# Cached keys in runs of 32 numbers, turned by VectorE in 32x32 blocks, in a hybrid decoder layer

## What is computed

```python
D_MODEL, SEQ, DEC_BATCH, DEC_SEQ, PAST_LEN, PAGE_SIZE = 1024, 512, 8, 4, 256, 128
h = rmsnorm(x, g_mix_pre)
q, k, v, xr, gb, gates = jnp.split(h @ w_in, [...], axis=-1)
k_all = jnp.concatenate([k_past.astype(k.dtype), k], axis=1)
v_all = jnp.concatenate([v_past.astype(v.dtype), v], axis=1)
...                              # logits = q.k * HEAD_DIM**-0.5 + bias; softmax; times v
o_rnn = hseq.astype(x.dtype) * jax.nn.gelu(gb)
merged = jax.nn.sigmoid(gate_a) * (o_attn @ w_pa) + jax.nn.sigmoid(gate_r) * (o_rnn @ w_pr)
x = x + rmsnorm(merged @ w_out, g_mix_post)
x = x + rmsnorm((jax.nn.silu(g_) * u_) @ w_down, g_ffn_post)
return x, k, v, new_conv, h_last
```

## Time and profile before

| | us |
|---|---|
| three runs | 796.84, 793.07, 792.98 |
| median | 793.07 |
| the profiled execution: its time | 796.87 |
| the profiled execution: its span | 795.1 |
| PE busy | 779.7 (98%) |
| DVE busy | 471.5 (59%) |
| ACT busy | 362.0 (46%) |
| POOL busy | 64.4 (8%) |

### The profile page before, as it was taken

The page is one execution under the profiler, slowest core; times in us unless marked ns, Lnnn a source line. Parts: engine busy times, 40 slices in busy tenths (PEclk is TensorE's granted clock), DMA queues, the critical chain, the costliest instruction groups (busy, mean ns, idle before and its releaser), DMA issues.

```text
span 795.1 us, 16472 instructions
## 1 busy us (share of the span) xinstructions
PE 779.7 (98%) x6116; PEld 739.2 (93%) x6116; DVE 471.5 (59%) x737; ACT 362.0 (46%) x628; POOL 64.4 (8%) x149
## 2 busy tenths in 40 slices
PE   8999999999999999999999999999999999999996
PEld 6988998899898899996789999999999999999996
DVE  4655746736646553674567987887777785222223
ACT  6345535625534732234455555455555564223232
POOL 3501102011010110004000000000000010000000
PEclk7999999999999999999999999999999999999998
DMA  7655244335422123625443333333333134223222
GB/s 212 176 167 162 82 119 137 96 106 150 119 79 81 53 80 112 212 80 179 159 137 84 91 114 92 89 91 106 106 106 106 53 130 127 77 74 91 87 58 113
DMA packets 148865, 89.21 MB, mean 112 GB/s; under 512 B 8709, under 2 KB 142297, under 8 KB 148826
## 3 DMA queue, kind: packets, MB, share of 16 engines
q1 hardware_dynamic: 146014, 81.63, 34.9%
q0 software_dynamic: 2576, 6.45, 2.5%
q10 hardware_dynamic: 236, 0.61, 0.3%
HBM read 81.85 MB, written 6.81 MB: 112 GB/s over the span
## 4 chain that ended last, share of the span: by engine, by line
PE 96%; DMA 1%; DVE 1%; ACT 1%; issue 1%; DVEq 0%; SPq 0%; ACTq 0%
PE ps L859 34%; PE ps L1204 26%; PE ps L1269 17%; PE ps L1103 6%; PE ps L1173 3%; PE ps L958 1%; PE ps L972 1%; PE ps L989 1%; PE ps L931 1%; DMA x_tok<-in_x_prompt_dram 1%; PE ps L881 1%; PE ps L1037 1%; PE ps L888 1%; PE ps L1111 1%; PE ps L1002 1%
## 5 line engine op out<-in xcount | busy, mean ns | idle before, releaser
L1818 DVE TENSOR_TENSOR w_lo<-w_raw,w_hi 128x1024 fp32r<-128x1024 f32 (+1 forms) x68 | 80.9, 1192 | 135.5 <-ACT w_hi L1346 135.2
L859 PE MATMUL ps<-xin_hi,w_hi 128*128 128x272 f32 x576 | 126.5, 299 | 0.9 <-DVE xin_lo L1841 0.9
L1346 ACT ACTIVATE w_hi<-w_raw 128x1024 fp32r<-128x1024 f32 (+1 forms) x68 | 69.9, 1030 | 118.7 <-PE ps L1269 82.6
L859 PE MATMUL ps<-xin_hi,w_lo 128*128 128x272 f32 x576 | 120.4, 288 | 0.0
L859 PE MATMUL ps<-xin_lo,w_hi 128*128 128x272 f32 x576 | 120.2, 288 | 0.0
L859 PEld LDWEIGHTS ps<-xin_hi,w_hi 128*128 128x128 f32 x576 | 90.1, 189 | 9.2 <-issue 7.6
L859 PEld LDWEIGHTS ps<-xin_lo,w_hi 128*128 128x128 f32 x576 | 91.0, 189 | 0.0
L859 PEld LDWEIGHTS ps<-xin_hi,w_lo 128*128 128x128 f32 x576 | 90.5, 189 | 0.0
L1269 PE MATMUL ps<-hid_hi,w_hi 128*128 128x272 f32 x352 | 76.0, 291 | 0.4 <-DVE hid_lo L2211 0.4
L1269 PE MATMUL ps<-hid_lo,w_hi 128*128 128x272 f32 x352 | 75.0, 287 | 0.0
L1269 PE MATMUL ps<-hid_hi,w_lo 128*128 128x272 f32 x352 | 74.9, 288 | 0.0
(11 more groups left out here) (340 smaller groups left out, 1766.0 us busy)
## 6 DMA issues: line engine op xcount, KB each, us to landing
w_raw<-in_w_in_dram SPq DMA_DIRECT2D x72, 256.0 KB, 3.1
g_raw<-in_w_gate_up_dram SPq DMA_DIRECT2D x40, 256.0 KB, 4.0
w_raw<-in_w_down_dram SPq DMA_DIRECT2D x40, 256.0 KB, 2.8
u_raw<-in_w_gate_up_dram SPq DMA_DIRECT2D x20, 256.0 KB, 3.0
e_raw<-in_w_gate_up_dram SPq DMA_DIRECT2D x20, 256.0 KB, 4.4
kc<-in_cache_k_dram SPq DMA_DIRECT2D x64, 64.0 KB, 2.1
vc<-in_cache_v_dram SPq DMA_DIRECT2D x64, 64.0 KB, 2.0
wo_raw<-in_w_out_dram SPq DMA_DIRECT2D x12, 256.0 KB, 4.1
```

Source lines behind the costliest of these rows:

```text
L859: mm = e.matmul(ps[:, bank + h, 0:HT], wt[:, kw, :], xt[:, kx, h * HT:h * HT + HT], start=first and wt is wh and xt is xh, stop=last and ( ...
L1346: e.activation((to or w_hi[s])[:, 0:k, :], w_raw[s][:, 0:k, :], ACT.Copy).then_inc(hi_done, count)
L1818: e.tensor_tensor(wl[:, 0:k, :], w_raw[s][:, 0:k, :], wh[:, 0:k, :].bitcast(F32), ALU.subtract).then_inc(lo_done, count)
```

## The change

Cached keys come from memory in another shape. A key DMA now takes its page slice as 4 blocks of 32 numbers by 128 tokens: block b goes to partitions 32b to 32b+31, `kc` is filled 128 x 4 x 32, in runs of 32 numbers (128 B), 512 runs for each DMA where there were 128 of 512 B. DVE turns four pages at once with its own transpose of 32x32 blocks (`keys_turn(f)`, 128x512), straight from `kc` to `kcT`. The first of the four waits for all 16 DMAs (`kc_in`), and in the loop for the last use of `prT` (`pv_done`). `cache_T` on PE and its copies on ACT and DVE are gone.

By this a page's token 4i + a comes to position 32a + i. The value pages are loaded with the same permutation of rows (4 groups of 32 tokens, still in runs of 512 B), and GpSimd copies the bias of the cached positions in that order, in four copies of 128x256 instead of one of 128x1024.

The prompt's keys go from `kT` to `tok` by one DVE transpose of 128x512, not by PE and ACT. Their store has 4 DMAs of 32 partitions in runs of 128 B where it had one in runs of 512 B. The stores wait for one step less of `mi_free`, counters are renumbered, and the semaphore `acc_zero` is replaced by another.

```diff
-            def load_pages(cache, dst, done, it, part):
+            def page_of(cache, it, j):
+                return cache[0].rearrange("n t h d -> n t (h d)")[bass.ds(page[j], 1), :, bass.ds(it * P, P)]
+            def load_keys(it, part):
                 for j in range(8 * part, 8 * part + 8):
-                    src = cache[0].rearrange("n t h d -> n t (h d)")[bass.ds(page[j], 1), :, bass.ds(it * P, P)]
-                    e.dma_start(dst[:, j, :], src.rearrange("o t c -> t (o c)")).then_inc(done, 16)
+                    e.dma_start(kc[:, j, :], page_of(cache_k, it, j).rearrange("o t (b c) -> b (o t) c", c=BLK)
+                                ).then_inc(kc_in, 16)
+            def load_values(it, part):
+                for j in range(8 * part, 8 * part + 8):
+                    e.dma_start(vc[:, j, :], page_of(cache_v, it, j).rearrange("o (i a) c -> a (o i) c", i=BLK)
+                                ).then_inc(vc_in, 16)
...
-                e.wait_ge(mi_free, it * 7 + 4)
+                        load_keys(it + 1, j - 5)
+                e.wait_ge(mi_free, it * 6 + 3)
                 for g, (op, os) in enumerate(((new_k_prompt, new_k_sample), (new_v_prompt, new_v_sample))):
-                    dst = op[0, 0].rearrange("(tt p) h d -> p tt (h d)", p=P)[:, :, bass.ds(it * P, P)]
-                    e.dma_start(dst, tok[:, g, 0:TT, :]).then_inc(kv_out, 16)
+                    if g == 0:
+                        for a in range(4):
+                            dst = op[0, 0].rearrange("(b i) h d -> i b (h d)", i=32)[:, :, bass.ds(it * P + 32 * a, 32)]
+                            src = tok[32 * a:32 * a + 32, g, 0:TT, :].rearrange("p tt (b j) -> p (tt b) j", j=32)
+                            e.dma_start(dst, src).then_inc(kv_out, 16)
...
-            e.tensor_copy(bias_s[:, :, 0:PAST], bias_rev[:, :, DEC_T:DEC_T + PAST][:, :, ::-1]).then_inc(consts, 1)
+            for f in range(PAIRS):
+                src = bias_rev[:, f, DEC_T:DEC_T + PAST][:, ::-1].rearrange("p (n i a) -> p n a i", n=NPG, i=BLK)
+                e.tensor_copy(bias_s[:, f, 0:PAST].rearrange("p (n a i) -> p n a i", n=NPG, i=BLK), src).then_inc(consts, 1)
...
-                def cache_T(f):
-
-                    if f == 0:
-                        e.wait_ge(kc_in, it * 256 + 256)
-                    tp_wait(f)
-                    for n in range(4):
-                        mm = e.transpose(ps[:, T_BANK, n * P:n * P + P], kc[:, 4 * f + n, :], ident[:, :])
-                    mm.then_inc(tp_ready, 1)
...
-                    begin(1); part(1, 0, 4); cache_T(0); part(1, 4, 8)
-                    cache_T(1); begin(2); part(2, 0, 2); cache_T(2); part(2, 2, 4); cache_T(3); part(2, 4, 8); scores_s()
+                    begin(1); part(1, 0, 8)
+                    begin(2); part(2, 0, 6); scores_s(); part(2, 6, 8)
                 else:
-                    begin(0); part(0, 0, 4); cache_T(0); part(0, 4, 8)
-                    begin(1); cache_T(1); part(1, 0, 4); cache_T(2); part(1, 4, 8)
-                    begin(2); cache_T(3); part(2, 0, 5); scores_s(); part(2, 5, 8)
+                    begin(0); part(0, 0, 8)
+                    begin(1); part(1, 0, 8)
+                    begin(2); part(2, 0, 5); scores_s(); part(2, 5, 8)
                 begin(3); scores(3); part(3, 0, 2); probs_T_s(); part(3, 2, 5)
-                tok_prompt(0, vT, 0, 3); probs_T(0); part(3, 5, 8)
-                begin(4); tok_sample(); probs_T(1); scores(2); part(4, 0, 3); tok_prompt(2, kT, 1, 2); part(4, 3, 5)
+                tok_values(); probs_T(0); part(3, 5, 8)
+                begin(4); tok_sample(); probs_T(1); scores(2); part(4, 0, 5)
...
-                e.activation(tok[:, 0, 0:TT, :], ps[:, M_BANK, :].rearrange("p (tt c) -> p tt c", c=P), ACT.Copy
-                             ).then_inc(mi_free, 1)
...
+                def keys_turn(f):
+                    if f == 0:
+                        e.wait_ge(kc_in, it * 256 + 256)
+                        if not first:
+                            e.wait_ge(pv_done, it)
+                    e.transpose(kcT[:, 2 * f:2 * f + 2, :].rearrange("p b k -> p (b k)"),
+                                kc[:, 4 * f:4 * f + 4, :].rearrange("p n c -> p (n c)")).then_inc(kc_turned, 1)
...
                     next_lo(0)
                     parameters()
-                    next_lo(1); cache_copy(1)
-                    k_copy(); cache_copy(3)
+                    keys_turn(0); keys_turn(1)
+                    next_lo(1)
+                    keys_turn(2)
+                    k_copy()
+                    keys_turn(3)
                     next_lo(2)
                 else:
-                    next_lo(0); cache_copy(1)
-                    next_lo(1); cache_copy(3)
-
+                    next_lo(0)
+                    keys_turn(0); keys_turn(1)
+                    next_lo(1)
+                    keys_turn(2); keys_turn(3)
                     next_lo(2)
                     k_copy()
...
+                e.transpose(tok[:, 0, 0:TT, :].rearrange("p tt c -> p (tt c)"), kT[:, 0:SEQ])
                 e.tensor_copy(tok[0:TS, :, TT, :], ps[0:TS, M_BANK, 0:2 * P].rearrange("p (g c) -> p g c", g=2)
```

More of the change, by code:

```diff
@@ L68 @@
 PT_USES = ((3, 0), (3, 1), (2, 0), (2, 1), (1, 2), (0, 2))
-TP_IT = 5 + len(PT_USES)
+TP_IT = 1 + len(PT_USES)
 TILES_IT = 8
@@ L92 @@
 C_ZERO = 8
-C_BIAS = C_ZERO + 1 + DEC_B + 2 * PAIRS
+C_BIAS = C_ZERO + PAIRS + DEC_B + 2 * PAIRS
+BLK = 32
 SERIES = 9
@@ L355, in program @@
         kc_in = sem("kc_in")
+        kc_turned = sem("kc_turned")
         vc_in = sem("vc_in")
@@ L450, in program @@
         ysq_used = sem("ysq_used")
-        acc_zero = sem("acc_zero")
         yt_ready = sem("yt_ready")
@@ L606, in iteration @@
                 if not last:
-                    e.wait_ge(mi_ready, it * 7 + 4)
-                    load_pages(cache_v, vc, vc_in, it + 1, 0)
-                    load_pages(cache_v, vc, vc_in, it + 1, 1)
+                    e.wait_ge(mi_ready, it * 6 + 3)
+                    load_values(it + 1, 0)
+                    load_values(it + 1, 1)
             load(2, 0, wi[:, :, 2 * 512:2 * 512 + P])
             for part in range(2):
-                load_pages(cache_k, kc, kc_in, 0, part)
+                load_keys(0, part)
             load(3, 1, wi[:, :, 3 * 512:3 * 512 + P])
@@ L937, in scores_s @@
                     e.wait_ge(tile_free[1], it * 4 + 2)
-                    e.wait_ge(mi_free, it * 7 + 1)
-                    tp_wait(4)
+                    e.wait_ge(mi_free, it * 6 + 1)
+                    e.wait_ge(kc_turned, it * 4 + 4)
                     e.wait_ge(logits_done, it * 9 + 1)
@@ L977, in probs_T_s @@
                     e.wait_ge(probs_done, it + 1)
-                    tp_wait(4)
+                    tp_wait(0)
                     for n in range(NPG):
@@ L1007, in out_s_T, with tok_values @@
                 def out_s_T():
-                    mi_wait(4)
+                    mi_wait(3)
                     e.transpose(ps[:, M_BANK, 0:P], o_s[:, :], ident[:, :]).then_inc(mi_ready, 1)
-                def tok_prompt(use, src, free, n_free):
-                    e.wait_ge(tile_free[free], it * 4 + n_free)
-                    mi_wait(use)
+                def tok_values():
+                    e.wait_ge(tile_free[0], it * 4 + 3)
+                    mi_wait(0)
                     for tt in range(TT):
-                        mm = e.transpose(ps[:, M_BANK, tt * P:tt * P + P], src[:, tt * P:tt * P + P], ident[:, :])
+                        mm = e.transpose(ps[:, M_BANK, tt * P:tt * P + P], vT[:, tt * P:tt * P + P], ident[:, :])
                     mm.then_inc(mi_ready, 1)
@@ L1029, in rg_gates @@
                         e.wait_ge(logits_done, it * 9 + 10)
-                    count = e.to_reg(it * 7 + (6 + h))
+                    count = e.to_reg(it * 6 + (5 + h))
                     e.wait_ge(consts, 2)
@@ L1394, in gate @@
                     e.activation(halves(dst), two(j % 2), ACT.Tanh, scale=0.5).then_inc(tile_free[j % 2], 1)
-                def cache_copy(f):
-                    e.wait_ge(tp_ready, it * TP_IT + (f + 1))
-                    e.activation(kcT[:, 2 * f:2 * f + 2, :], ps[:, T_BANK, :].rearrange("p (b k) -> p b k", b=2),
-                                 ACT.Copy).then_inc(tp_free, 1)
                 def exp_s():
@@ L2282, in _ @@
             e.wait_ge(q3_done, NS)
-            e.memset(yacc[:, :], 0.0).then_inc(acc_zero, 1)
-            e.wait_ge(acc_zero, 1)
+            e.memset(yacc[:, :], 0.0).then_inc(consts_v, 1)
+            e.wait_ge(consts_v, 4)
             def down_lo(n, odd, c):
```

53 lines of the change are left out of this document (24 added, 29 removed).

## The result

The changed kernel takes 827.13 us (median of four runs, 825.71 to 828.5), the kernel before 793.06. The ratio is 1.041, 95% interval 1.038 to 1.044. The prediction said 848, in a range of 803 to 915.

What follows compares the result with a forecast made beforehand. PE bounds the kernel before (98% busy); after, the queue on four engines: 34.6 us later to iteration 2's key issue, 20.4 for two further periods, less 0.4, is 54.6, so 793.1 becomes 847.7 (848), range 803 to 915.

Steps and rivals of the forecast that it cites:

- engines from the outermost dimension: Key and value loads: a load is spread over its outermost dimension, 4 here, so both run on 4 engines of 16.
- The 43 packets of q10: Queue q10's packets beyond 193 of data, read as completion packets, 16 + 11 + 16, one for each engine a load uses.
- The first wait: Iteration 0, before tile 2: DVE waits for all 16 key DMAs and PE stands idle for 14.6 us.
- its vanishing in the queue: Iteration 0: the 14.6 us are no term of their own, because the four engines stay full from there.
- the waits before tile 0: Loop: PE idle before tile 0, whose weights land 52 us after a key issue; period 74 us against 64.
- before tiles 6 and 7: Loop: PE idle before these tiles too, as their weights queue behind key loads on four engines; period 74 us against 64.
- The price of a 128 B packet: Key loads and stores: 13.5 ns a packet, from a line through 512 B (29.1 ns) and 4096 B (174.9 ns).
- 8.6 us for a nanosecond: Whole kernel: each nanosecond of a 128 B packet adds 8.2 us by four key batches, 8.6 with the stores.
- Rival C: Same queue, but the clock falls after new gaps: tile 0 takes 11.2 us instead of 8.0, time 857; chance 0.15.
- A: Rival: all 16 engines serve the new loads, a key batch takes 6.9 us, hidden; 784.7 us, faster; chance 0.08.
- B: Rival: 128 B packets cost about what 512 B packets cost, 22 ns and more; up to 982 us; chance 0.10.
- D: Rival: PE still stands for something else where groups were removed, so they give nothing; 793 us; chance 0.01.

Runs made afterwards that it cites:

- no_first_wait: Changed kernel, but in iteration 0 DVE turns a gain row instead of the cached keys and waits for no key page; all DMAs stay: 826.2 us.
- best2: Changed kernel, but iteration 0 loads and turns keys as before; values in token order, half issued behind the next iteration's tile 0; DVE writes keys in token order: 786.6 us.
- keys_512B_4: Changed kernel, but a key DMA takes whole rows of 512 B, 128 packets in 4 groups of 32 tokens, on four engines: 801.2 us, ratio 1.009.
- both_16: Changed kernel, but values in token order and keys in whole 512 B rows, both on 16 engines, PE reading cached keys with a stride: 789.5 us, ratio 0.993.

## Why the prediction held, and what was mis-sized

**The step that decided, engines from the outermost dimension, is shown**: by the paces at 16, 4 and 2 engines and by the completion packets. The 43 packets of q10 were enough to tell.

**The signs and places.** The first wait (13.3 against 14.6), its vanishing in the queue, and the waits before tile 0 came as forecast. The waits that the prediction put before tiles 6 and 7 show within the tiles: PE's wait for ACT's `ti` at 93.07 stands behind a `w_hi` that waited 4.95 us for its weights. PE was busy for 94% where 91% was forecast.

**The price of a 128 B packet was too high: 13.5 ns.** Eight key DMAs in 9.69 us are 1.21 each, 9.5 ns for each of 128 packets; in the first batch, 22.65 / 16 gives 11.1. By the prediction's own 8.6 us for a nanosecond, 9.5 instead of 13.5 takes 34.4 us off: 847.7 becomes 813.3.

The windows tell which step was wrong. In the first only key packets of the changed kernel move (with a few completion packets), in the second only its value packets, both on four engines of 16 (us, busy times, granted clock, DMA share, GB/s).

```profile
204.00:208.00 4.00, 4.00 (x36) 3.99 (x35) 2.96 (x10) 1.89 (x7) 0.00 (x0) 1.00 0.35 54
93.00:98.00 5.00, 4.93 (x42) 4.40 (x44) 1.74 (x2) 3.13 (x6) 0.00 (x0) 1.00 0.29 78
```

By the prediction's method, share x 16 x bytes / GB/s, a 128 B packet is busy for 0.35 x 16 x 128 / 54 = 13.3 ns: its line was nearly right. But four engines of 16 can be busy for a share of 0.25 at most if each takes one packet after another, and the share is 0.35 and 0.29. So the packets of one engine overlap, and one starts every 4 x 128 / 54 = 9.5 ns. The prediction took the time that a packet is busy for the time that it costs the queue. A share of 1.09 in the earlier trace rows had said as much. The same goes for 512 B: 0.29 x 16 x 512 / 78 = 30 ns busy, 4 x 512 / 78 = 26 apart (24.5 in the run on two engines), where 29.1 was taken.

The estimate that the prediction drew from the Trainium skill, 10.7 ns ("DMA: Bandwidth & Descriptors", section "Why small descriptors are slow (HBM only)"), was nearer. For the values the error was small: from their first issue at 90.91 to the landing of tile 0 at 108.61 it is 17.7 us, where the forecast had 14.9 + 1.9 + 1.9 = 18.7.

**What lies between 813 and 827.** The tile 0 of iteration 1 lands at 108.6 where 9.5 ns gives 122.5 - 16.9 = 105.6: 3.0 us, about what the dearer first batch costs (16 x 128 x 1.6 ns = 3.3). From that landing to tile 1's start it is 119.75 - 108.61 = 11.1, not 10.2, and 11.6 from there to the key issue, not 11.4: 1.2 us. Keys of iteration 2 are issued 21.9 us late by the trace (131.40 - 109.52), where the forecast had 34.6. Each further period is 68.4 and 67.6 against 64.2, 4.3 and 3.4 later, where 9.5 ns would give 65.8 and 1.6: 2.7 and 1.8 more. Together 3.0 + 1.2 + 2.7 + 1.8 = 8.7.

Of the other 5 us, 1.4 are the changed kernel's profiled execution, which lies below its median. 3.8 are a fault in how the sum was set up. The forecast counted iteration 0 by the clock, from the key issue on, and subtracted a trace of before in which the slow prologue had made PE late; then it added the difference to a median of executions that are 3.8 us shorter. The late start was in only one of the two. In the changed kernel such a start hardly shows, because the queue sets the end of the iteration: the profiled execution of no_first_wait had it (0.51 from 11.8 to 22 us) and took 825.97 us, between its others.

So 827 lies as near to 848 as it does because these 14 us stand against the 34 of the price. That part was luck. The upper bound of 915 is also a little more than its own terms give (21 ns is 912, 20 ns with C 914).

**Rival C came in part.** Windows of the changed kernel (us, busy times, granted clock, DMA share, GB/s):

```profile
46.44:50.60 4.16, 4.16 (x19) 4.16 (x20) 2.90 (x4) 1.06 (x1) 0.00 (x0) 0.53 0.44 140
50.60:55.00 4.40, 4.40 (x44) 3.67 (x44) 0.47 (x2) 0.05 (x1) 0.00 (x0) 1.00 0.50 143
111.10:116.00 4.90, 4.90 (x24) 4.90 (x25) 4.05 (x7) 3.54 (x5) 0.42 (x2) 0.58 0.39 108
179.30:184.00 4.70, 4.70 (x25) 4.70 (x26) 3.77 (x6) 3.57 (x5) 0.08 (x1) 0.64 0.39 113
```

After each wait PE works at or near the lower level, 1.2 GHz, for some 4 to 5 us: 19 matmuls in 4.16 us, and 44 in the 4.40 behind. The mechanism was right, its price not: it was to cost 3.2 us before each key issue, and the path from tile 0's landing to tile 1's start is longer than the forecast by 0.9 us in iteration 1 (11.1 against 10.2) and 1.2 in iteration 2 (188.19 - 176.75 = 11.4), since most of tile 0 lies beside DVE's tail there. That these are the clock's is argued; no run separates them.

**Rivals A, B and D fell**: A by the paces and the packet counts, B because 128 B costs under half of what 512 B does (9.5 against 24.5 ns), D because best2's period is shorter by its five groups.

## What to carry to other kernels

Before a transpose is moved from PE to the shape of a load, look at the outermost dimension that the load gets: four blocks outermost leave it four engines, and all that is queued behind on those four waits for it, weights included. A queue that is full sets its own end, so removing the largest single wait in the profile can bring nothing; add up the service of the queue, not the waits. Take what a packet costs from a stretch in which the engines that serve it are full, as bytes over time; a busy share counts packets that overlap twice. A slow load is free where a period of SP's queue has room and nothing urgent stands behind it.

## What the runs showed of the hardware that I had not expected

- SP is held by a queue that is full. Of 16 value DMAs on four engines the first eleven issue in 0.55 us each and the last four in 0.74, and key DMAs go from 0.6 to a steady 1.0:

```profile
97.46 0.55 SPq L581
98.11 0.59 SPq L581
98.81 0.74 SPq L581
99.64 0.74 SPq L581
```

- A packet of 128 B costs one engine 9.5 to 11 ns, one of 512 B 24.5 to 26 and, in the first batch of keys_512B_4, some 30, by what else moves. Each is busy for longer than that (13.3 and 30 ns in the windows above), since packets on one engine overlap.
- A matmul of 256 columns that reads its moving operand in jumps of 128 B takes 620 ns against 379, and a group of 16 takes 2.0 us against 1.0. DVE's 32x32 transpose of 128x512 takes 0.69 us and, written with a distance of 16 B, 1.09.
- The clock of the prologue differs between executions: in the profiled one of before PE ran for 10 us at 0.53, in that of the changed kernel not at all, after 1.09 us of idle time at the same place instead of 1.88. The idle time doesn't sort them: both_16 had 0.30 us there, and its clock was 0.83 from 11.8 to 22 us.
